# One GpSimd instruction per weight chunk, and a masked decay table for the scan

## The reference

```
p = RMSNorm(x) @ w_in            # q, kv, rope key, z, x/B/C, dt, two gates
A = latent attention             # 16 heads, prompt and 8 cached rows
B = conv + SSD scan + gated RMSNorm   # 32 heads in 8 groups, chunks of 128
mix = (sig(ga) * (A @ w_a) + sig(gb) * (B @ w_b)) @ w_out
x = x + RMSNorm(mix);  x = x + RMSNorm(W_down relu(W_up RMSNorm(x))^2)

cs = cumsum(dt * a) within a chunk                       # per head
decay[l, s] = exp(cs[l] - cs[s]) for l >= s, else 0
y = (C B^T * decay) (x dt) + C state exp(cs);  state = state exp(cs_last) + ...
```

## Time and profile before

| what | value |
|---|---|
| median of 3 runs | 1735.67 us (1730.96 to 1737.14) |
| the profiled execution | 1737.14 us, its span 1735.4 us |
| PE busy | 1507.0 us, 87% |
| DVE busy | 897.7 us, 52% |
| ACT busy | 512.1 us, 30% |
| POOL busy | 584.4 us, 34%, of it L413 572.3 us in 736 instructions |
| PE L572, L623 | 256 and 64 passes, 36.9 and 10.8 us busy |
| mean granted PE clock | 0.921 |

### The profile page before, as it was taken

The page is one execution under the profiler, slowest core; times in us unless marked ns, Lnnn a source line. Parts: engine busy times, 40 slices in busy tenths (PEclk is TensorE's granted clock), DMA queues, the critical chain, the costliest instruction groups (busy, mean ns, idle before and its releaser), DMA issues.

```text
span 1735.4 us, 29329 instructions
## 1 busy us (share of the span) xinstructions
PE 1507.0 (87%) x11936; PEld 1395.7 (80%) x11936; DVE 897.7 (52%) x1794; ACT 512.1 (30%) x930; POOL 584.4 (34%) x748
## 2 busy tenths in 40 slices
PE   5899889799797998988987688999993999999995
PEld 4898778788686887878876467778992999999995
DVE  5567577666775775757767532221326222222225
ACT  3233323323233232332332222222222322222231
POOL 2353332233322323323231013223443444454541
PEclk9889989899898998998988788998996999999997
DMA  3123122122211212212213069863320222223221
GB/s 111 61 89 102 52 77 73 40 89 69 83 62 41 89 61 68 85 52 85 66 42 109 4 187 291 258 207 116 135 86 13 86 89 94 92 92 98 89 95 62
DMA packets 109591, 160.51 MB, mean 92 GB/s; under 512 B 16497, under 2 KB 83570, under 8 KB 109458
## 3 DMA queue, kind: packets, MB, share of 16 engines
q1 hardware_dynamic: 56594, 130.14, 23.1%
q10 hardware_dynamic: 52864, 28.51, 5.8%
HBM read 145.87 MB, written 12.74 MB: 91 GB/s over the span
## 4 chain that ended last, share of the span: by engine, by line
PE 69%; DVE 20%; ACT 3%; issue 3%; ACTq 2%; SPq 1%; POOL 1%; DMA 1%; DVEq 0%; POOLq 0%
PE lin L456 51%; PE Pb L487 2%; PE lin L631 2%; PE lin L495 2%; PE Pb L543 2%; ACTq L1027 1%; PE lin L605 1%; DVE acc L1467 1%; PE Pb L552 1%; PE lin L572 1%; PE Pb L584 1%; PE Pb L587 1%; PE Pb L559 1%; DVE arena L1363 1%; PE Pb L725 1%
## 5 line engine op out<-in xcount | busy, mean ns | idle before, releaser
L413 POOL TENSOR_TENSOR w_lo<-w_stage,w_hi 128x256 fp32r<-128x256 f32 x736 | 572.3, 808 | 1102.7 <-ACT w_hi L826 1102.7
L456 PE MATMUL lin<-act_hi,w_hi 128*128 128x260 f32 x1760 | 372.4, 294 | 22.0 <-DVE acc L1535 9.0
L456 PE MATMUL lin<-act_lo,w_hi 128*128 128x260 f32 x1760 | 360.9, 287 | 0.0
L456 PEld LDWEIGHTS lin<-act_hi,w_hi 128*128 128x128 f32 x1760 | 279.1, 195 | 31.4 <-issue 22.7
L456 PEld LDWEIGHTS lin<-act_lo,w_hi 128*128 128x128 f32 x1760 | 279.5, 194 | 0.0
L826 ACT ACTIVATE w_hi<-w_stage 128x1024 fp32r<-128x1024 f32 x184 | 193.9, 1054 | 252.2 <-PE lin L456 217.5
L456 PE MATMUL lin<-mid_hi,w_hi 128*128 128x260 f32 x1024 | 217.2, 295 | 35.7 <-DVE mid_lo L1456 16.4
L456 PE MATMUL lin<-act_hi,w_lo 128*128 128x260 f32 x1760 | 233.9, 285 | 0.0
L456 PEld LDWEIGHTS lin<-act_hi,w_lo 128*128 128x128 f32 x1760 | 219.9, 189 | 3.3 <-issue 3.3
L456 PE MATMUL lin<-mid_lo,w_hi 128*128 128x260 f32 x1024 | 212.4, 290 | 0.0
L456 PEld LDWEIGHTS lin<-mid_hi,w_hi 128*128 128x128 f32 x1024 | 165.1, 198 | 46.5 <-issue 36.0
(11 more groups left out here) (238 smaller groups left out, 1992.8 us busy)
## 6 DMA issues: line engine op xcount, KB each, us to landing
w_stage<-in_wall SPq DMA_DIRECT2D x184, 512.0 KB, 3.7
arena<-in_cache SPq DMA_DIRECT2D x124, 144.0 KB, 3.2
arena<-in_state ACTq DMA_DIRECT2D x16, 512.0 KB, 7.2
out_stateT<-arena ACTq DMA_DIRECT2D x16, 512.0 KB, 4.0
o_attn<-in_cache SPq DMA_DIRECT2D x64, 128.0 KB, 3.5
o_attn<-in_cache ACTq DMA_DIRECT2D x64, 128.0 KB, 3.9
arena<-in_xT SPq DMA_DIRECT2D x8, 520.0 KB, 5.6
out_yT<-arena SPq DMA_DIRECT2D x8, 260.0 KB, 2.0
```

The lines of the kernel that those rows point to most:

```text
L413: low = pool.tensor_tensor(w_lo[:, slot, part], w_stage[:, slot, part], w_hi[:, slot, part].bitcast(F32), ALU.subtract)
L456: mm = pe.matmul(lin[:, pl.slot, hf, 0:HALF], w[:, ch.slot, off:off + P], r[:, hf * HALF:(hf + 1) * HALF], start=(k == 0 and p == 0), stop ...
```

## The change

The change has three parts. POOL splits a chunk in one instruction of 1024 columns instead of four of 256. The one-hot weights of L572 and L623 are gone: DVE builds `csm` (the 32 rows of `cs3` times the one-hot columns of the group, side by side for 4 heads, 32x512) and `sdm` (the same for the 16 sample columns, 32x64), and PE multiplies them by `ones` in one matmul each. DVE writes `sdm` and `csm` of chunk 0 at a group's start and `csm` of chunk c+1 behind Cx of chunk c. PE waits for `sdm_ready` and `csm_ready`, and no longer for `state_ready`, `rows_ready` and `sp_ln` ahead of the sample decay.

```diff
@@ split
-                        for q in range(4):
-                            part = slice(256 * q, 256 * q + 256)
-                            low = pool.tensor_tensor(w_lo[:, slot, part], w_stage[:, slot, part],
-                                                     w_hi[:, slot, part].bitcast(F32), ALU.subtract)
-                        low.then_inc(S["w_split"], 1)
+                        pool.tensor_tensor(w_lo[:, slot, :], w_stage[:, slot, :], w_hi[:, slot, :].bitcast(F32),
+                                           ALU.subtract).then_inc(S["w_split"], 1)
@@ PE
-                def head_row(h):
-                    return ident[0:32, 4 * g + h:4 * g + h + 1].to_broadcast([32, P])
                 def scan_front(c):
                     free_slot(pl)
+                    pe.wait_ge(S["csm_ready"], g * 4 + (c + 1))
-                    for h in range(HPG):
-                        pe.matmul(lin[:, pl.slot, 0, h * P:(h + 1) * P], head_row(h), cs3[:, tok], start=True, stop=True)
+                    pe.matmul(lin[:, pl.slot, 0, :], ones[0:32, :], csm[:, :, :], start=True, stop=True)
...
-                if g:
-                    pe.wait_ge(S["state_ready"], g * 4)
-                else:
-                    pe.wait_ge(S["rows_ready"], 1)
-                    pe.wait_ge(S["sp_ln"], 2)
-                for h in range(HPG):
-                    mm = pe.matmul(Pb[:, 3, 16 * h:16 * h + 16], head_row(h), cs3[:, SEQ:SEQ + 16], start=True, stop=True)
-                mm.then_inc(S["sdec_mm"], 1)
+                pe.wait_ge(S["sdm_ready"], g + 1)
+                pe.matmul(Pb[:, 3, 0:64], ones[0:32, :], sdm[:, :, :], start=True, stop=True
+                          ).then_inc(S["sdec_mm"], 1)
@@ DVE
+                onehot = ident[0:32, bass.ds(g * 4, 4)]
+                def masked_decay(c):
+                    dve.tensor_tensor(csm[:, :, :], repeat(cs3[:, CHUNK * c:CHUNK * (c + 1)], HPG),
+                                      spread(onehot, CHUNK), ALU.mult).then_inc(S["csm_ready"], 1)
@@ scan_front on DVE, behind Cx
+                    if c < NCH - 1:
+                        masked_decay(c + 1)
@@ start of a group with rest
+                dve.tensor_tensor(sdm[:, :, :], repeat(cs3[:, SEQ:SEQ + 16], HPG), spread(onehot, 16), ALU.mult
+                                  ).then_inc(S["sdm_ready"], 1)
+                masked_decay(0)
```

More of the change, by code:

```diff
@@ L149 @@
     hist_in conv_out raw_act conv_acc conv_tanh xc_ready qbd_hi_s q_ready k_act v_act
-    sdec_mm st_in0 st_in1 st_new st_out0 st_out1 scores max_bias exp_done prob_ready
-    pt_done pt_ready pv_done o_ready a_row a_seg a_exp b_ready y_done state_ready state_out
+    sdm_ready sdec_mm st_in0 st_in1 st_new st_out0 st_out1 scores max_bias exp_done prob_ready
+    pt_done pt_ready pv_done o_ready csm_ready a_row a_seg a_exp b_ready y_done state_ready state_out
     yg_ready sqg_ready g_stat g_diag g_val g_hi g_ready z_tanh groups_over
@@ L201, in build_layer @@
         cs3 = sb("cs3", [SSM_HEADS, SEQ + 16])
+        csm = sb("csm", [SSM_HEADS, HPG, CHUNK])
+        sdm = sb("sdm", [SSM_HEADS, HPG, 16])
         sdec = sb("sdec", [P, 2, 16])
```

## The result

The changed kernel took 1798.3 us (median of 4 runs, 1794.1 to 1803.8), the kernel before 1735.5 beside it: ratio 1.037, 95% interval 1.033 to 1.040. It is slower by some 63 us; forecast were 37, and 1748 to 1803 as the range.

What follows compares the result with a forecast made beforehand. PE, plus what DVE adds between PE's work, bounds the kernel. Seven steady groups at 3.0 us (21), rows 8.4, big product 2 and last group 0.2 make +31.6; clock +6: 1773 us for the median, range 1748 to 1803.

Steps and rivals of the forecast that it cites:

- POOL's hold: On the shared SBUF port, DVE is kept out for one whole POOL instruction of 1024 columns, 2.15 us.
- Last stretch: End of a steady group: L1282 ends later, L1467 and PE go with it, +1.75 us per group.
- Chunk 1: Scan chunk 1 of a steady group: csm and normalise stand behind POOL, PE's L552 starts 1.89 us later.
- Chunk 2: Scan chunk 2 of a steady group: csm and normalise stand behind POOL, PE's L552 starts 0.58 us later.
- Chunk 0: Scan chunk 0 of a steady group: L1415, starting DVE's chain to the next scores, moves by 0.45 us.
- The first big product: The pair of L1403 in a group: the first waits 1.6 us for POOL, the second not at all; +2 in all.
- The clock: Grown PE waits bring one 3.4 us stretch at 1.2 GHz per group, taken at half price: +6 us.
- The order hardly matters: Scan chunks 0 to 2: csm getting in ahead of POOL would cost about 2.5 us rather than 2.9.
- Rival C: Every grown wait, the row phase's too, brings a stretch at 1.2 GHz: 20 x 1.5 us more, 1803; chance 12%.
- Rows: Row phase: the first L1501 loses the port to POOL, the pair costs +1.4 us, six rows: +8.4.
- Sample decay: Sample rows on PE: two passes of 64 columns replace eight of 16, gaining 1.0 us per group.
- The last group: No weight stream there: three csm cost 2.0 us on DVE against 1.4 + 0.4 gained on PE, +0.2.

Runs made afterwards that it cites:

- the run with half the fill: Changed kernel plus PE matmuls that compute nothing, 8 and 6 ahead of the odd transposes in scan chunks 1 and 2: 1784.7 us, ratio 1.027.

## Why the prediction was right in direction and low in size

- *POOL's hold* (2.15 us for 1024 columns): right. 2.16 for csm (2.83 - 0.67), 2.0 for L1273, 2.1 for L1503. The Trainium skill's rule ("SBUF — State Buffer", section "Who interferes with whom") that the pair is locked for a whole instruction is borne out by the four csm rows; its second half, that the first issued wins, holds in chunk 0 (POOL 0.37 us earlier) and not in chunk 1 (0.01 us earlier).
- *Last stretch* +1.75: L1273 ended 1.6 us later. *Chunk 1* +1.89: normalise ended 1.8 later. *Chunk 2* +0.58: it ended 0.5 later. Right within 0.2 us. *Chunk 0* +0.45: nothing, POOL got in ahead of Cx there and csm found the port free.
- *The first big product* (L1403, now L1405) +2 in all: it waits 1.6 us as forecast. With the clock up, the stretch to the first spread takes 13.9 us, and 12.8 with the tables and short pieces; with the clock down it is the same in both. Two of six groups had it up: about right.
- *The clock* (+6, one stretch of 3.4 us per group at half price) is the step that failed; the mechanism was right and the term too small. The clock fell behind both waits of the scan and behind the last stretch's, each in three or four of six groups, and cost about 1.5 us each time. By that count it is some 2.5 a group, 17 to 18 us over seven, 12 of them in the scan; the run with half the fill gained 17 (10 to 24) there. The groups are not alike in this, as the prediction takes them to be: the six spans took 110.5 to 113.8 us before and 116.6 to 119.1 after. The forecast had taken at most two per group at 1.7 as its upper bound, and then a quarter of that.
- *"The order hardly matters"* speaks of who gets the port first, csm or POOL, both behind Cx; no run sets that. What the runs do show is what csm's place in DVE's program is worth, of which the prediction says nothing: 35 us (25 in the groups of the traces). PE waits 1.0 us more in chunk 1 (2.59 against 1.60) and 0.9 in chunk 2 (2.00 against 1.12), and behind these longer waits the clock can fall, for 1.46 and 0.87 in the group shown, while it stays up behind the shorter ones. The waits were in the forecast's sum; the clock behind them was there with too little.
- *Rival C*, every grown wait with a stretch at 1.2 GHz, gave nearly the right time, 1803, and had part of the reason: the clock falls at the waits of the row phase too, but not at each. From the first L1501 (L1503) to the last, in the kernel before and in the changed kernel:

```profile
1052.20:1193.80 141.60, 134.68 (x1336) 112.33 (x1335) 39.36 (x147) 32.59 (x60) 39.24 (x56) 0.99 0.74 232
```

```profile
1107.90:1254.50 146.60, 136.42 (x1336) 113.87 (x1335) 46.71 (x146) 32.23 (x60) 33.33 (x14) 0.97 0.70 221
```
- *Rows* +8.4: the pair costs 1.3 each as forecast, six times (16.5 us of L1503 in all, 8.7 before). The phase took 5 us more in this trace. The other five traces with one POOL instruction in the rows took 149.7 to 151.8 us at a clock of 0.94 to 0.97, the other five with four pieces 138.2 to 139.8 at 0.99 or 1.00. So the term is right or a little small, the clock comes on top there too, and the 5 us of this pair of traces are at the low end. *MLP* 0: right.
- *Sample decay* -1.0: 0.9 in the trace (1.29 us from L623 to what follows it, 0.43 from L614), 9 to 16 us over eight groups by sdm alone. *Scan spread* -0.44: nothing.
- *The last group* +0.2: +8 in the profiled run. Three csm of 0.60 us net are 1.8 of it. The rest is at a clock of 0.50 without a break. A window of the changed kernel there, one of the kernel before, and one of the tables with eight short pieces:

```profile
978.80:1009.50 30.70, 23.75 (x90) 16.73 (x91) 19.81 (x44) 7.37 (x21) 0.00 (x0) 0.50 0.11 35
```

```profile
935.90:966.60 30.70, 20.42 (x119) 15.84 (x119) 22.23 (x51) 9.76 (x28) 0.00 (x0) 0.78 0.11 35
```

```profile
913.70:944.40 30.70, 23.87 (x91) 16.84 (x92) 19.81 (x45) 7.38 (x21) 0.00 (x0) 0.50 0.11 35
```

90 passes kept PE busy for 23.8 us, where 119 had taken 20.4. The long POOL instruction is not the cause: with eight short pieces the window is the same, and the stretch from the last rope product to the row phase takes 142.9 us, as against 143.9 in the changed kernel and 132 to 140 in the other traces. Both traces have the tables, and so have eight in which it did not happen; what decides it is open.

## What to carry to other kernels

An engine that is off the chain can still lengthen it through a port: split its long SBUF instructions where the other engine's two-input instructions want the port, and read on to the wait that ends behind a held one: a held COPY of 0.15 us cost PE nothing here, the big product after it did. Work added for a second engine belongs into that engine's idle time, not between its last input and the result that PE waits for: the same instruction cost some 35 us in one place and next to nothing in the other. A wait that grows on PE (here from 1.6 to 2.6 us) can cost the clock of the passes behind it as well; passes that compute nothing can be the cheaper filling, if they are shorter than the wait.

## What the runs showed that was not expected

- Useless PE work made the kernel faster: 17 us in two waits of the changed kernel's scan, 11 us at the norm of the kernel before. Twice as much in the scan gave the gain back.
- A POOL subtraction of 128x1024 takes 2.38 to 2.44 us where it gets the port at once, and 2.9 where DVE's Cx has it; four of 256 take 3.2 and eight of 128 3.9 (709.0 us over 184 chunks), and the kernel with the slowest POOL is the fastest of the four.
- The same wait of PE (2.59 us) was followed by a fall of the clock in four groups and by none in two. So the groups of the changed kernel differ by up to 2.5 us (116.6 to 119.1), although these waits are alike.
- The spread as one fp32 matmul over 512 columns (two passes) is no faster than four over 128 with eight loads: 1.12 against 1.08 us.
